# Two shared rings for weight landing buffers and split halves in a hybrid decoder step, with two-chunk expert transfers

## The reference, cut to what matters

```python
def layer(i, h, ...):
    h = h + mixer(rmsnorm(h, norm1[i]), ..., w_in[i], ..., w_o[i])      # w_in 1024x2560, w_o 1024x1024
    hn = rmsnorm(h, norm2[i])
    f = swiglu(hn, gate, up, down) if i % 2 == 0 else moe(hn, router, wg, wu, wd)
    h = h + f                                                           # 2816 wide, or 8 experts of 1408
    gate = sigmoid(h @ w_ple_gate[i]); e = p_l @ w_ple[i]               # 1024x1024, 256x1024
    return h + gate * e

def moe(x, ...):
    for e in range(8):
        y = y + gates[..., e:e+1] * swiglu(x, wg[e], wu[e], wd[e])      # 1024x1408 twice, 1408x1024
```

## Time and profile before

| | |
|---|---|
| time, median of 3 runs (us) | 1034.43 (1032.98 to 1040.81) |
| the profiled execution (us) | 1032.9, of which 1031.1 are its span |
| busy: PE, DVE, ACT, POOL (us) | 942.6, 720.1, 521.0, 142.2 |
| mean granted TensorE clock | 0.959 |
| mean transfer rate over the span | 218 GB/s, 224.86 MB in all |

### The profile page before, as it was taken

How to read it: one execution, slowest core, us unless ns; L and a number is a source line. 1 busy time by engine, 2 the same in 40 slices (tenths; PEclk the granted TensorE clock), 3 DMA queues, 4 the chain that set the end, 5 groups by cost and what they waited for, 6 DMA issues and landing times.

```text
span 1031.1 us, 14724 instructions
## 1 busy us (share of the span) xinstructions
PE 942.6 (91%) x6081; PEld 813.9 (79%) x6081; DVE 720.1 (70%) x821; ACT 521.0 (51%) x538; POOL 142.2 (14%) x176
## 2 busy tenths in 40 slices
PE   4999999999999989999889898998989799898974
PEld 4999899999999989988767586676757577575774
DVE  3785576555655778746677776976878777887853
ACT  5421454443444443224566656755666655766442
POOL 4226121101100453432000000000000000000013
PEclk9999999999999999989899899998999999999987
DMA  9944155586458476322488869896789959898801
GB/s 325 308 133 130 37 169 164 141 250 202 119 164 270 135 190 214 111 77 90 138 303 294 303 221 336 285 355 234 253 314 305 338 192 312 308 323 330 304 3 43
DMA packets 120823, 224.86 MB, mean 218 GB/s; under 512 B 5906, under 2 KB 90002, under 8 KB 120608
## 3 DMA queue, kind: packets, MB, share of 16 engines
q1 hardware_dynamic: 118688, 216.63, 62.6%
q0 software_dynamic: 2064, 7.23, 2.7%
HBM read 220.31 MB, written 3.99 MB: 218 GB/s over the span
## 4 chain that ended last, share of the span: by engine, by line
PE 54%; DMA 16%; DVE 15%; ACT 8%; issue 5%; POOL 2%; SPq 0%; DVEq 0%; ACTq 0%; POOLq 0%
PE bank L607 12%; PE bank L608 12%; PE bank L609 12%; DVE wlo L1250 9%; DMA raw<-in_moe_w_down 6%; ACT whi L1025 5%; DMA raw<-in_moe_w_up 5%; DMA raw<-in_moe_w_gate 4%; PE bank L880 2%; PE bank L881 2%; PE bank L882 2%; PE bank L798 1%; PE bank L799 1%; DVE hid L1540 1%; ACT hid L1107 1%
## 5 line engine op out<-in xcount | busy, mean ns | idle before, releaser
L1250 DVE TENSOR_TENSOR wlo<-raw,whi 128x1408 fp32r<-128x1408 f32 (+2 forms) x254 | 478.5, 1892 | 156.0 <-ACT whi L1025 154.3
L1025 ACT ACTIVATE whi<-raw 128x1408 fp32r<-128x1408 f32 (+2 forms) x254 | 395.6, 1567 | 203.5 <-PE bank L609 56.1
L607 PE MATMUL bank<-xh,whi 128*128 128x264 f32 x672 | 195.6, 291 | 14.7 <-DVE xl L1262 14.7
L608 PE MATMUL bank<-xl,whi 128*128 128x264 f32 x672 | 192.5, 286 | 0.0
L609 PE MATMUL bank<-xh,wlo 128*128 128x264 f32 x672 | 192.1, 286 | 0.0
L854 PE MATMUL bank<-whi,xeh 128*96 128x512 f32 (+1 forms) x384 | 145.1, 378 | 5.9 <-ACT hid L1107 2.9
L856 PE MATMUL bank<-whi,xel 128*96 128x512 f32 (+1 forms) x384 | 144.6, 377 | 0.0
L855 PE MATMUL bank<-wlo,xeh 128*96 128x512 f32 (+1 forms) x384 | 144.1, 375 | 0.0
L607 PEld LDWEIGHTS bank<-xh,whi 128*128 128x128 f32 x672 | 128.7, 191 | 16.7 <-DVE wlo L1250 10.9
L608 PEld LDWEIGHTS bank<-xl,whi 128*128 128x128 f32 x672 | 128.8, 192 | 0.3
L609 PEld LDWEIGHTS bank<-xh,wlo 128*128 128x128 f32 x672 | 128.1, 191 | 0.0
(11 more groups left out here) (225 smaller groups left out, 1380.4 us busy)
## 6 DMA issues: line engine op xcount, KB each, us to landing
raw<-in_moe_w_gate SPq DMA_DIRECT2D x64, 704.0 KB, 5.8
raw<-in_moe_w_up SPq DMA_DIRECT2D x64, 704.0 KB, 5.5
raw<-in_moe_w_down SPq DMA_DIRECT2D x40, 1024.0 KB, 7.6
raw<-in_w_in SPq DMA_DIRECT2D x20, 1024.0 KB, 9.6
raw<-in_ffn_w_down SPq DMA_DIRECT2D x16, 704.0 KB, 4.6
raw<-in_ffn_w_gate SPq DMA_DIRECT2D x10, 1024.0 KB, 5.7
raw<-in_ffn_w_up SPq DMA_DIRECT2D x10, 1024.0 KB, 5.4
raw<-in_w_o SPq DMA_DIRECT2D x8, 1024.0 KB, 5.6
```

The lines of the kernel that those rows point to most:

```text
L607: pe.matmul(out, w_hi, x_hi, start=start, stop=False)
L608: pe.matmul(out, w_hi, x_lo, start=False, stop=False)
L1025: act.activation(whi[u % SPL][:, 0:n], raw[u % RAW][:, 0:n], ACT.Copy).then_inc(hi_ready, 1)
L1250: dve.tensor_tensor(wlo[u % SPL][:, 0:n], raw[u % RAW][:, 0:n], whi[u % SPL][:, 0:n].bitcast(F32), ALU.subtract).then_inc(lo_ready, 1)
```

## The change

The four-slot buffers become two rings counted in columns, in the same 24,576 columns of memory. One ring of 17,408 columns holds raw values and lower halves: `raw` and `wlo` are two names (and types) of the same memory, and DVE writes the lower half over the raw values. The other, of 7,168 columns, holds the upper halves. A unit takes as many columns as it has; where it doesn't fit before the ring's end, it starts at 0. From the rings follow two waits. A transfer waits until PE has used the last unit that lies where it will land (`LOAD_AFTER`, never less than for the transfer before it); the upper half of unit u waits until PE has used unit `HIGH_LAST[u]`.

In the expert stage one gate or up transfer brings two chunks, that is two units, in the order gate k, gate k+1, up k, up k+1, and PE uses them in that order. A down transfer still brings two chunks, but each chunk is a unit of 1024, so a down phase has 11 units instead of six; the steps' numbers in `GATHER_AFTER`, `HID_AFTER` and `LAST_SCATTER_AFTER` are changed so that they stand behind the same chunks. ACT and DVE split unit v at the step `SPLIT_AT` gives: as early as the upper ring allows, with at most 5,632 columns between the unit in use and v. `silu_gate` waits for 14 units of the phase where it waited for 15. The steps `ahead` with `AHEAD = 2` in the dense stages stay.

```diff
-RAW = 4
-SPL = 4
+LOW_COLS, HIGH_COLS = 17408, 7168
+LANDINGS = 16
+LOOK = 5632
...
-DOWN = ((0, 2), (2, 2), (4, 2), (6, 2), (8, 2), (10, 1))
+DOWN = EC
...
+def ring(sizes, room):
+    at, taken, out = 0, [], []
+    for n in sizes:
+        if at + n > room:
+            at = 0
+        last = max((i for i, (a, b) in enumerate(taken) if a < at + n and at < b), default=-1)
+        out.append((at, last))
+        taken.append((at, at + n))
+        at += n
+    return out
...
+LOW_RING = ring([sum(COLS[u:u + n]) for u, n in LOADS], LOW_COLS)
+HIGH_AT, HIGH_LAST = zip(*ring(COLS, HIGH_COLS))
...
+def split_table():
+    out, first = {}, U_FF[1]
+    for v in range(first + AHEAD, U_PLE[1] + AHEAD):
+        u = max(HIGH_LAST[v] + 1, first)
+        while sum(COLS[u:v]) > LOOK:
+            u += 1
+        out.setdefault(min(u, U_PLE[1] - 1), []).append(v)
+    return out
...
-GATHER_AFTER = {0: 0, 2: 1, 3: 2, 4: 3}
-HID_AFTER = {1: (2, 0), 3: (1,)}
+GATHER_AFTER = {1: 0, 5: 1, 7: 2, 9: 3}
+HID_AFTER = {3: (2, 0), 7: (1,)}
...
-        raw = [place(f"raw{i}", [P, UNIT]) for i in range(RAW)]
-        whi = [place(f"whi{i}", [P, UNIT], F32R) for i in range(SPL)]
-        wlo = [place(f"wlo{i}", [P, UNIT], F32R) for i in range(SPL)]
+        low_at = at[0]
+        raw = place("raw", [P, LOW_COLS])
+        wlo = place("wlo", [P, LOW_COLS], F32R, low_at)
+        whi = place("whi", [P, HIGH_COLS], F32R)
...
-                if vector_through is not None:
-                    sp.wait_ge(lo_ready, vector_through)
...
+                if LOAD_AFTER[i]:
+                    sp.wait_ge(unit_used, LOAD_AFTER[i])
...
-                        for k in range(DC):
+                        for k in range(0, DC, 2):
                             for i, src in enumerate((gate, up)):
...
+                                load(u + 2 * k + 2 * i, src[k * P:(k + 2) * P, :], 2, FE)
...
-                k, up = divmod(i, 2)
+                k, up = i // 4 * 2 + i % 2, i // 2 % 2
...
-                act.wait_ge(raw_landed[u % RAW], 16 * (u // RAW + 1))
-                if u >= SPL:
-                    act.wait_ge(unit_used, u - (SPL - 1))
...
+                act.wait_ge(raw_landed[i % LANDINGS], 16 * (i // LANDINGS + 1))
+                if HIGH_LAST[u] >= 0:
+                    act.wait_ge(unit_used, HIGH_LAST[u] + 1)
+                act.activation(unit_hi(u), unit_raw(u), ACT.Copy).then_inc(hi_ready, 1)
...
-                act.wait_ge(unit_used, U_FF[1] + MOE_AT["gu", e] + GU_UNITS - 1)
+                act.wait_ge(unit_used, U_FF[1] + MOE_AT["gu", e] + GU_UNITS - 2)
```

More of the change, by code:

```diff
@@ L215, with add_load @@
 N_UNITS = U_MIX[DEPTH]
+PART_COLS = [(DC if kind != "down" else EC) * w * P for kind, _, w, _, _ in PART]
+COLS, LOADS = [], []
+def add_load(*cols):
+    LOADS.append((len(COLS), len(cols)))
+    COLS.extend(cols)
+for _l in range(DEPTH):
+    for _spec in W_IN + W_O:
+        add_load(_spec[2] * _spec[4])
+    if _l == 0:
+        for _w in PART_COLS * 2:
+            add_load(_w)
+    else:
+        for _kind, _e in PHASES:
+            if _kind == "gu":
+                for _ in range(DC):
+                    add_load(FE, FE)
+            else:
+                for _f in range(0, EC, 2):
+                    add_load(*[D] * min(2, EC - _f))
+    for _spec in PLEU:
+        add_load(_spec[2] * _spec[4])
+assert len(COLS) == N_UNITS
+def ring(sizes, room):
[10 more added lines that the diff above has]
+HIGH_AT, HIGH_LAST = zip(*ring(COLS, HIGH_COLS))
+LOW_AT, LANDING, LOAD_AFTER = [], [], []
+for _i, (_u, _n) in enumerate(LOADS):
+    _at, _last = LOW_RING[_i]
+    LOAD_AFTER.append(max(sum(LOADS[_last]) if _last >= 0 else 0, *LOAD_AFTER[-1:], 0))
+    for _j in range(_n):
+        LOW_AT.append(_at)
+        LANDING.append(_i)
+        _at += COLS[_u + _j]
+    assert _i < LANDINGS or LOAD_AFTER[_i] >= sum(LOADS[_i - LANDINGS])
+def split_table():
[6 more added lines that the diff above has]
+    return out
+SPLIT_AT = split_table()
 def chunk_table():
@@ L427, in program @@
         bank = [ctx.enter_context(nc.psum_tensor(f"bank{i}", [P, 512], F32)) for i in range(8)]
-        raw_landed = [sem(f"raw_landed{i}") for i in range(RAW)]
+        raw_landed = [sem(f"raw_landed{i}") for i in range(LANDINGS)]
         hi_ready, lo_ready, unit_used = sem("hi_ready"), sem("lo_ready"), sem("unit_used")
@@ L495, in h_final, with unit_raw, unit_lo, unit_hi @@
                 eng.wait_ge(acc_free, first + m + 1)
[L498 to L506, removed]
+        def unit_raw(u):
+            return raw[:, LOW_AT[u]:LOW_AT[u] + COLS[u]]
+        def unit_lo(u):
+            return wlo[:, LOW_AT[u]:LOW_AT[u] + COLS[u]]
+        def unit_hi(u):
+            return whi[:, HIGH_AT[u]:HIGH_AT[u] + COLS[u]]
         def y_bank(e):
@@ L547, in feed_forward @@
                         src = {"gate": gate, "up": up, "down": down}[kind]
-                        load((n.unit + i) % RAW, n.unit + (i - RAW + 1), src[:, c * P:(c + w) * P],
-                             EC if kind == "down" else DC, w * P)
+                        load(n.unit + i, src[:, c * P:(c + w) * P], EC if kind == "down" else DC, w * P)
             def experts():
@@ L555, in experts @@
                     if kind == "gu":
[L556 removed]
+                        for k in range(0, DC, 2):
                             for i, src in enumerate((gate, up)):
[L558 to L562 removed]
+                                load(u + 2 * k + 2 * i, src[k * P:(k + 2) * P, :], 2, FE)
+                    else:
+                        for f in range(0, EC, 2):
+                            n = min(2, EC - f)
+                            load(u + f, down[f * P:(f + n) * P, :], n, D)
             dense(0, U_MIX[0], W_IN[:1])
@@ L871, in down @@
                     pe.wait_ge(hid_ready, 3 * NE)
[L872 to L882, removed]
+                if i % 4 == 0:
+                    pe.wait_ge(hl_ready, hid_turn(e, i // 4) + 1)
+                X, Y = hh[:, hid_slot(e, i), :], hl[:, hid_slot(e, i), :]
+                for half in range(2):
+                    b = bank[y_bank(e) + half][0:CAP, :]
+                    own = slice(half * 512, (half + 1) * 512)
+                    pe.matmul(b, X, H[:, own], start=(i == 0), stop=False)
+                    pe.matmul(b, X, L[:, own], start=False, stop=False)
+                    mm = pe.matmul(b, Y, H[:, own], start=False, stop=(i == EC - 1))
                 mm.then_inc(unit_used, 1)
@@ L892, in experts @@
                 for kind, e in PHASES:
-                    for i in range(GU_UNITS if kind == "gu" else len(DOWN)):
+                    for i in range(GU_UNITS if kind == "gu" else DOWN):
                         if kind == "gu":
@@ L1122, in experts @@
                 for kind, e in PHASES:
-                    for i in range(GU_UNITS if kind == "gu" else len(DOWN)):
-                        split_next(MOE_AT[kind, e] + i + SPL - 1)
+                    for i in range(GU_UNITS if kind == "gu" else DOWN):
+                        split_next(U_FF[1] + MOE_AT[kind, e] + i)
                         if kind == "gu":
```

78 lines of the change are left out of this document (37 added, 41 removed).

## The result

The changed kernel takes 982.9 us (median of 4 runs, 982.3 to 983.6) against 1034.5 for the kernel before, measured beside it: ratio 0.949, 95% interval 0.945 to 0.953. The profiled execution has a span of 980.6 us at a mean granted clock of 0.972, against 1031.1 at 0.959.

What follows compares the result with a forecast made beforehand. No engine was full in the experts; a loop of transfer, upper half, lower half, next transfer over four raw slots held them. Sum: 1032.9 - 51.5 (expert stage) + 10 (embedding part) = 991.4, said as 991 us; range 974 to 1022.

Steps and rivals of the forecast that it cites:

- PE's own need in the stage: Expert stage: PE's matmuls, gathers, slot values, transposes and scatters need 409.6 us at the full clock, of 471.5.
- Stalls left in the stage: Expert stage: of today's 62 us of stalls, 10 remain (bounds 4 and 20), making the stage 420 us.
- the lower bound of 4: Expert stage: 4 us of stalls remain if only phase-end hand-offs are left.
- the hand-offs: Expert phase ends: PE waits while DVE ends the hidden rows, 0.5 us in each of seven phases.
- Late landings cost nothing: Experts: a pair lands in 7.5 us against 7.6 of lead at the tightest; landings up to 4 us late cost nothing.
- Lower halves in place cost nothing, DVE is hidden: Experts: in-place adds have no price; DVE's 372 us become 378, 92% of PE's 410, hidden behind PE.
- The embedding part: Layer 0's embedding part: upper halves of gate units 1 and 2 wait for PE; layer 1 begins 10 us later (4 to 13).
- The dense stages: Dense stages: the upper ring of three units instead of four slots costs nothing; bounds 0 and +4 in `w_in`.
- the slower rival: Dense stages: with an upper ring of three, PE waits for free banks, up to +87 us, 1078 us; chance 0.07.
- Transfers bind: Experts: transfers queued deeper go no faster, 310 GB/s, stage 438 instead of 420 us, 1009 us in all; chance 0.18.
- It doesn't do what it says: Experts: the stall moves from lower halves to landings; the stage gains only the embedding part's 10 us, 1033 us; chance 0.08.

Runs made afterwards that it cites:

- run 9: Changed kernel with LOOK 4224 and rings of 17024/7552 (970.8 us) or 16384/8192 columns: 971.4 us with layer 0's sigmoids moved ahead of the next upper half, 969.5 without.
- run 5: Changed kernel with halves made at most 4224 columns ahead (LOOK) instead of 5632: 980.7 us, ratio 0.945 to the kernel before.
- run 3: Changed kernel with a lower ring of 11264 columns instead of 17408, expert transfers mostly 6 units ahead: 1013.5 us, ratio 0.979 to the kernel before.
- run 8: Changed kernel with rings of 16384 and 8192 columns, so the upper ring holds four units of 2048 instead of three: 972.3 us, ratio 0.940 to the kernel before.
- run 6: Changed kernel with the third of three products left out of the experts' gate, up and down matmuls: 945.8 us in one run.
- run 1: Changed kernel with 384 columns moved from the lower to the upper ring (17024 and 7552): 973.6 us, ratio 0.939 to the kernel before.
- run 7: Changed kernel with, in layer 0's embedding part, the upper half of the unit two ahead made behind the pair of sigmoids: 979.9 us, ratio 0.947 to the kernel before.
- run 2: Changed kernel with a lower ring of 8448 columns instead of 17408, expert transfers mostly 4 units ahead: 1178.6 us, ratio 1.137 to the kernel before.

## Why the prediction was right, step by step

The forecast was 991 us and the kernel takes 982.9, within the range. Both large terms have the sign and place forecast; one was mis-sized.

- *PE's own need in the stage, 409.6 us.* Right to 1 us: with PE never idle (run 9) the stage takes 408.6 to 408.7.
- *Stalls left in the stage, 10 us.* This is the term that failed: "Between these bounds I take 10, nearer to the lower, since the rest too is mostly ACT and DVE held up behind landings". Measured: 411.4 - 409.6 = 1.8 us (2.8 against run 9's 408.6), below the lower bound of 4. The reason given for a value above 4 was itself a reason for the lower bound: landings no longer hold up ACT at all, so the rest went with the waits. The stage came out at 411.4 instead of 420: 8.6 of the 9.0 us between the sum, 991.4, and the profiled execution's 982.4. Of the hand-offs, put at 0.5 us in each of seven phases, 1.6 us were left, and they came from halves made too early (run 5).
- *Late landings cost nothing.* Right: pairs landed in 7.3 to 7.7 us against the estimate of 7.5. They cost at 6 units of lead (run 3) and not at mostly 8 (run 8); the change has mostly 10 to 12.
- *Lower halves in place cost nothing, DVE is hidden.* Right: 1616 and 1217 ns against 1621 and 1220. DVE's work is 372.7 us, not 378, and stands at 90% of the stage, not 92; it is the next bound (run 6).
- *The embedding part, +10 us.* Right in size and mechanism: +10.95 at layer 1, +10.4 at the experts; first gate matmul 342.87 against 342.1, table load to 353.8 against 352.8, next upper half 357.89 against 356.5. Run 1 shows that the ring's wrap is the cause. Of the 11 us, 4.9 are PE's late first gate matmul and 6.0 come behind it; run 7 gives the sigmoids' place about 2 of these 6.0, and how the other 4 divide between PE's later feed, its lower clock and DVE's order was not taken apart.
- *The dense stages, 0.* Right (run 8), so the slower rival falls. *Transfers bind* falls with 327 GB/s over the stage, 413 to 418 at best, and no landing waited for. The Trainium skill's 358 GB/s ("DMA: Bandwidth & Descriptors", section "Where 436 GB/s comes from") was no bound: 418 GB/s over 10 us. Its page "Perfetto Trace Analysis" (section "Roofline") says that a core working alone may pass that share up to some 435; the runs here agree. *It doesn't do what it says* falls too, though run 2 shows the same code 14% slower than before when the ring is short: in place, storage comes free only when PE is done with it, where before it came free after the lower half, so the in-place ring needs its depth. The wait moved from lower halves to landings there, as this rival said; it is the depth that keeps it away.

## What to carry to other kernels

A prefetch ring has a loop (landing, the passes over the data, the use) and a depth; divide the one by the other and compare with the pace of the engine that should bound. It is a first estimate, not a model: it came within 7 us of the stage in runs 2 and 3, with the landing times of those very runs. From 4 to 6 units of lead the stage fell by 150 us, from 6 to mostly 8 by 28, and beyond that by nothing. When a stall's cause goes, ask of each remaining stall whether it hung on the same cause before carrying it over into the sum. In a ring of units of different widths, tabulate for every unit which earlier one it lies on: one wrap cost 11 us here, and 384 columns moved from one ring to the other gave back 9.

## What had not been expected of the hardware

- Transfers ran at 413 and 418 GB/s for 10 us with PE, DVE and ACT all at work, above the 368 and 399 of the earlier trace rows; with two products (run 6) they held 370 GB/s for 365 us.
- The time from issue to landing is no constant of the size. A 1408 KB transfer took 6.1 to 6.2 us (medians) in run 2, where the stage ran at 232 GB/s, 6.8 to 7.7 in run 3 (313 GB/s), 7.3 to 7.7 in the change (327), and 8.7 to 8.8 in run 6 (370). It rose with the rate; the cause was not tested.
- In run 2 PE's granted clock over the stage was 0.90, in the change 0.99: PE's waits cost twice there, once idle and once at the lower level behind them (from 713 to 718 us the granted clock is 0.50, and a matmul of 512 columns follows the one before it by 0.43 us; from 719 to 723 it is 1.00, and they follow by 0.23).
